# First mixer in a new order, distance biases as stacked fp32r products ahead of both mixers, and input loads on the weight queue

## Chip, cores, metric

The kernel runs on one core of a Trainium2 chip. The metric is the time of one execution in device microseconds; three runs of the kernel before the change gave a median of 3287.96 us. TensorE does the matrix products, VectorE (DVE) and ScalarE (ACT) the elementwise work, GpSimd (POOL) elementwise work and some DMA issues, SyncE (SP) issues the weight loads.

## What is computed

The reference runs two blocks one after the other on one sequence of 256 tokens with 1024 features. The first block has a mixer AB, an expert layer, a mixer C and another expert layer; the second has two gated mixers, each followed by a retrieval layer. The change touches mixer AB and the start of mixer C.

```python
def mixer_ab(x, w_in, gate_b, conv_w, head_g, w_out, rel_bias):
    p = einsum('bsd,de->bse', x, w_in)      # aq ak av (8 heads of 64), bq bk bv bo (4 heads of 128), bi bf
    qk = silu(causal_conv(p[..., AB_BQ:AB_BV], conv_w))
    ya = dilated_attention(aq, ak, av, rel_bias)          # softmax(q k / 8 + bias(distance)) v
    yb = sigmoid(bo) * head_norm(mlstm(bq, bk, bv, bi, bf), head_g)
    return einsum('bse,ed->bsd', concatenate([ya, yb]), w_out)
# mlstm per head, with b = cumsum(log_sigmoid(f)):
#   P = exp(D - m),  D[t,s] = b[t] - b[s] + i[s] for s <= t,  m = max(b + 0, max_s D)
#   h = (q k' * P) v / max(|sum_s (q k' * P)|, exp(-m))
# mixer_c: three attentions over 8 heads; its logits add rel_bias[bucket(distance)] too,
#   those of the compressed keys at the distances t - (16 n + 31), n = 0..14
```

## The kernel before

Every weight product is made in fp32 accuracy from two fp32r parts: a weight tile of 128 x 1024 is loaded by SP into one of three raw buffers (`rawb`), split in halves of 512 columns into a high part (`splitb`, ScalarE, `split_half` at L481) and a low part (`raw - high`, L504, by GpSimd or VectorE, as the field `lo` of `stream_order` says), and TensorE makes three products of each (high-high, high-low, low-high). The five base buffers of split halves form a ring: a half is split when the half five places before it has been used. The order of weight tiles is one list (`stream_order`); each engine's program goes through the stages in the same order, and `fed(n)` in an engine's program splits the halves that the next n tiles free. So the order on each engine is written by hand, and every instruction waits only for counters.

A distance bias (`Bias`) is built by TensorE: the table `relp` (32 buckets and a row of ones), repeated over 128 columns, times a 0/1 matrix `ohm` (33 x 512), plain fp32 operands in `arena`, one product for each of 8 heads. ScalarE copies each to `tmp` (2 buffers), GpSimd writes it to DRAM (`skew`), and one load with a slanted pattern reads it back as `B`. Each mixer does this at its own start, before its first weight product. Mixer C also makes 30 products of 8 columns for the compressed keys (`ohc`, `Bc`).

Mixer AB goes: 16 transposes of x (`Start`), 8 bias products, 8 tiles `aq` (`proj`, 24 products of 256 columns each), 8 tiles `ab_v` (`rows`, 12 products of 512 columns each), the gate inputs (`Narrow`, 48 products), then attention A in 8 steps (score, softmax, transpose, mix, one after the other) with the 8 convolved tiles `bq` between, then the mLSTM in 8 cells of its own chain with the 8 tiles `ab_o` between, the head norm on VectorE, 16 transposes of y and 8 tiles `ab_out`. `aq`, `ab_v`, `bq`, `ab_o` and `ab_out` name tiles below; `hH`, `hL` are high and low parts of the transposed activations. Norm follows, then the expert layer.

Of the kernel before, what the change touches and what calls it, by code (L numbers as in the profile page):

```python
# [25 lines left out]
AB_AUX = dict(conv=32, gateb=8, headg=512, rel=8, wif=64)  # L26
C_AUX = dict(gateb=24, pos=64, rel=8, wg=192)
# [180 lines left out]
def stream_order(dram):  # L208
# [222 lines left out]
class Sync(Lane):  # L431
    def program(self, S):
        group = None
        for n, (src, _, lo, ring) in enumerate(S.order):
# [348 lines left out]
class Start:  # L783


# [3 lines left out]
    def act(self, act):  # L789
        S = self.S  # L790
        act.load("cst", S.cst[:, :], S.dram["consts"])
        act.load("x", S.hrow, S.dram["x_rows"])
        act.load("rt", S.rt[:, :], S.dram["router"])
        for t in range(2):
            take_transposes_act(act, S, t, "xT")

    def dve(self, dve):
        dve.fill(self.S.eps, EPS, ("eps",))
        for t in range(2):
            take_transposes_dve(dve, self.S, t, "xT")  # L800

    def pe(self, pe):
        S = self.S
        pe.wait_ge(S.load("cst"), "cst")
        pe.wait_ge(S.load("x"), "x")
        for t in range(2):
            pe.transposes(S.hrow[:, t, :], t, "xT")

    def pool(self, pool):
        pass  # L810
# [26 lines left out]
class Bias:  # L837


    def __init__(self, S, layer, B, relp, ohm, tmp, table):  # L840
        self.S, self.layer, self.B, self.relp, self.ohm, self.tmp = S, layer, B, relp, ohm, tmp
        self.table = table

    def act(self, act):
        S, n = self.S, self.layer
        for h in range(8):
            act.wait_ge(S.product, "bias", n, h)
            if h >= 2:
                act.wait_ge(S.load(f"skew{n}_{h - 2}"), "skew")
            act.cp(self.tmp[:, h % 2, :], S.bank["bias", n, h], ("bias", n, h), ("drained", ("bias", n, h)))  # L850

    def dve(self, dve):
        dve.fill(self.relp[32:33, :, :], 1.0)
        dve.cp(self.relp[0:32, :, :], bc(self.table, 2, 128), ("rel", self.layer))

    def pe(self, pe):
        S, n = self.S, self.layer
        pe.wait_ge(S.vdone, "rel", n)
        pe.wait_ge(S.load(f"ohm{n}"), f"ohm{n}")
        for h in range(8):  # L860
            b = pe.open("bias", n, h)
            pe.out(pe.mm(b, self.relp[0:33, h, :], self.ohm, True, True), ("bias", n, h))

    def pool(self, pool):
        S, n = self.S, self.layer
        for h in range(8):
            pool.wait_ge(S.acted, "bias", n, h)
            sig = S.load(f"skew{n}_{h}")
            pool.eng.dma_start(S.skew.ap()[n, h, :, :], self.tmp[:, h % 2, :]).then_inc(sig.sem, sig.step(("skew",)))
        for h in range(8):  # L870
            pool.wait_ge(S.load(f"skew{n}_{h}"), "skew")
        sig = S.load(f"B{n}")
        src = bass.AP(S.skew, n * 8 * 65536 + 127, [[511, 128], [65536, 8], [1, 256]])
        pool.eng.dma_start(self.B, src).then_inc(sig.sem, sig.step(("B",)))
# [27 lines left out]
class MixerAB:  # L902
    HEADS = [(h, t) for h in (0, 2, 4, 6) for t in range(2)]
    CELLS = [(h, t) for h in range(4) for t in range(2)]

    def __init__(self, S):
        self.S = S
        R = Room(S.arena)
        self.aux = S.aux_views(AB_AUX)
        self.B = R.get(8, 256)  # L910
        relp = R.get(8, 128)
        self.ohm = R.get(512)
        tmp = R.get(2, 512)
# [8 lines left out]
        self.rcol = R.get(2, 4)  # L922
        self.l2 = [R.get(512) for _ in range(3)]
        self.p2 = [R.get(512) for _ in range(3)]
        self.lp = [R.get(256) for _ in range(4)]
        self.pt = [R.get(256) for _ in range(4)]
        self.dgb = [R.get(256) for _ in range(2)]
        self.small = [R.get(16) for _ in range(8)]
        self.small2 = [R.get(16) for _ in range(8)]
        self.w8 = R.get(2, 4)  # L930
        self.hn = R.get(2, 4, 32)
        self.cmask = R.get(256)
        self.bias = Bias(S, 0, self.B, relp, self.ohm[0:33, :], tmp, self.aux["rel"][0:32, :])
        self.narrow = Narrow(S, self.aux["wif"], 8, "ab.if")

    def pe(self, pe):
        S = self.S
        self.bias.pe(pe)
# [3 lines left out]
        pe.rows(1024, "rows", "ab.v")  # L942
        self.narrow.pe(pe)
        b = pe.open("ab.b")
# [5 lines left out]
        for k, j in steps(8, 3, 8):  # L950
            if k == 0:
                self.pe_score(pe, j)
            elif k == 1:
                self.pe_turn(pe, j)
            elif k == 2:
                self.pe_mix(pe, j)
            else:
                i = CONV[j]
                pe.proj(pe.open("bq", i)[:, 0:256], ("bq", i))
        for t in range(2):  # L960
            pe.wait_ge(S.acted, "ab.v", t, 0)
        for k, j in steps(8, 3, 8):
            if k == 0:
                self.pe_mscore(pe, j)
            elif k == 1:
                self.pe_mturn(pe, j)
            elif k == 2:
                self.pe_mmix(pe, j)
            else:
                pe.row_step(j, 8, 512, "rows", "ab.o")  # L970
        pe.wait_ge(S.vdone, "ab.y")
        for t in range(2):
            pe.transposes(self.y[:, t, :], t, "ab.yT")
        pe.rows_T = ("ab.yT",)
        pe.wait_ge(S.acted, "ab.o", 1)
        pe.rows(1024, "rows", 0)
# [24 lines left out]
    def pe_mix(self, pe, j):  # L1001
        S = self.S
        h, t = self.HEADS[j]
        ns = 128 * (t + 1)
        p = self.p2[j % 3]
        b = pe.open("ab.x", j)
        pe.wait_ge(S.acted, "ab.p", j)
        pe.wait_ge(S.acted, "ab.v", 1, 1)
        for a in range(2):
            for i in range(t + 1):  # L1010
                ins = pe.mm(b[:, 64 * a:64 * a + 64], p[:, ns * a + 128 * i:ns * a + 128 * i + 128],
                            self.vv[:, i, 64 * (h + a):64 * (h + a) + 64], i == 0, i == t)
        pe.out(ins, ("ab.x", j))

    def pe_mscore(self, pe, j):
        S = self.S
        h, t = self.CELLS[j]
        ns = 128 * (t + 1)
        b = pe.open("ml.s", j)
        pe.wait_ge(S.vdone, "ml.d", j)  # L1020
        pe.out(pe.mm(b[:, 0:ns], S.ones, self.dgb[j % 2][:, 0:ns], True, True), ("ml.d", j))
        pe.wait_ge(S.acted, "bqk")
        pe.out(pe.mm(b[:, 256:256 + ns], self.bqk[:, h, 128 * t:128 * t + 128], self.bqk[:, 4 + h, 0:ns],
                     True, True), ("ml.s", j))

    def pe_mturn(self, pe, j):
        S = self.S
        h, t = self.CELLS[j]
        b = pe.open("ml.t", j)
        pe.wait_ge(S.vdone, "ml.w", j)  # L1030
        for i in range(t + 1):
# [1802 lines left out]
```

## Time and profile before

| | us |
|---|---|
| median of 3 runs | 3287.96 (3286.97 to 3293.88) |
| the profiled execution | 3281.58 |
| its span, first to last instruction | 3279.80 |
| of that, from the start to the end of mixer AB | 225.98 |
| of that, mixer C, from its first product to the Norm behind it | 640.59 to 857.80 |

The profiled execution is 6.4 us shorter than the median. Times in the trace count from the first instruction. The granted clock is a share of 2.4 GHz: 1.00 is 2.4, 0.50 is 1.2.

### The profile page before, as it was taken

To read this page: it belongs to the slowest core of one execution; us is meant where nothing else is said; L and a number is where in the kernel's file an instruction comes from. 1 tells how busy PE (TensorE), PEld (TensorE's weight loads), DVE (VectorE), ACT (ScalarE), POOL (GpSimd) and SP (SyncE) were. 2 spreads that over 40 slices of the span, in tenths; PEclk is the share of its full clock that TensorE was granted. 3 is DMA by queue.
4 is the path that set the end of the run, shared out by engine and by line. 5 is a ranking of instruction groups with operands and counts; after the bars stand their busy time and mean duration, and the time that the engine had idled before them with its cause. 6 is when DMAs were issued, how large, how long until landed. Compare 5 with 4: busy or idle time off the path is not lost.

```text
span 3279.8 us, 48648 instructions
## 1 busy us (share of the span) xinstructions
PE 3053.8 (93%) x17834; PEld 2663.9 (81%) x17834; DVE 2214.4 (68%) x3863; ACT 1855.0 (57%) x2824; POOL 1137.7 (35%) x1046
## 2 busy tenths in 40 slices
PE   7769999898899997989999999999989999999998
PEld 6647888586688885789999988887779999988887
DVE  0448999504589995569665557776569855557777
ACT  4446888424578884544555555555555555555554
POOL 6321000132200002569767620001568867630000
PEclk8879999789899998999999999999999999999999
DMA  5237999443489992346665567776345665567775
GB/s 186 71 117 267 370 368 371 177 139 109 160 334 368 372 371 85 103 148 201 192 187 184 183 224 242 242 241 215 104 141 188 204 184 184 181 222 241 242 243 201
DMA packets 203808, 702.01 MB, mean 214 GB/s; under 512 B 23633, under 2 KB 24017, under 8 KB 203155
## 3 DMA queue, kind: packets, MB, share of 16 engines
q1 hardware_dynamic: 170784, 617.69, 56.5%
q10 hardware_dynamic: 20724, 41.36, 3.5%
q0 software_dynamic: 12064, 39.86, 3.1%
q8 instruction: 144, 2.36, 0.3%
q14 instruction: 92, 0.75, 0.1%
HBM read 660.01 MB, written 38.80 MB: 213 GB/s over the span
## 4 chain that ended last, share of the span: by engine, by line
PE 85%; DVE 6%; POOL 3%; ACT 2%; DMA 2%; issue 1%; ACTq 0%; DVEq 0%; SPq 0%; POOLq 0%
PE ps L552 84%; POOL splitb L504 3%; PE ps L563 2%; DVE hrow L104 1%; DVE arena L104 1%; DVE arena L94 1%; ACT splitb L481 1%; DVE arena L99 1%; ACT arena L158 1%; ACT L158 1%; DMA rawb<-in_peer_u 0%; DMA rawb<-in_cmp_w 0%; DVE hL L94 0%; ACT arena L160 0%; DMA rawb<-in_peer_v 0%
## 5 line engine op out<-in xcount | busy, mean ns | idle before, releaser
L481 ACT ACTIVATE splitb<-rawb 128x512 fp32r<-128x512 f32 x1328 | 833.0, 631 | 950.1 <-PE ps L552 795.6
L504 POOL TENSOR_TENSOR splitb<-rawb,splitb 128x512 fp32r<-128x512 f32 x632 | 854.8, 1369 | 1389.2 <-ACT splitb L481 1378.2
L552 PE MATMUL ps<-hH,splitb 128*128 128x256 f32 x5248 | 987.3, 287 | 16.7 <-POOL splitb L504 16.2
L552 PEld LDWEIGHTS ps<-hH,splitb 128*128 128x128 f32 x5248 | 837.6, 194 | 22.5 <-ACT splitb L481 10.6
L552 PE MATMUL ps<-splitb,hid 128*128 128x512 f32 x3444 | 791.9, 390 | 10.8 <-issue 10.8
L552 PEld LDWEIGHTS ps<-splitb,hid 128*128 128x128 f32 x3444 | 648.8, 188 | 147.2 <-issue 11.2
L504 DVE TENSOR_TENSOR splitb<-rawb,splitb 128x512 fp32r<-128x512 f32 x696 | 484.2, 714 | 414.6 <-ACT splitb L481 413.9
L552 PE MATMUL ps<-hL,splitb 128*128 128x256 f32 x2624 | 748.3, 285 | 0.0
L552 PEld LDWEIGHTS ps<-hL,splitb 128*128 128x128 f32 x2624 | 509.6, 194 | 0.0
L552 PE MATMUL ps<-experts_r 128*128 128x512 f32 (+1 forms) x1348 | 332.8, 398 | 14.9 <-ACT experts_r L158 8.5
L552 PEld LDWEIGHTS ps<-experts_r 128*128 128x128 f32 x1348 | 254.9, 196 | 69.9 <-ACT experts_r L158 7.5
L2602 POOL DMA_DIRECT2D aux<-spill x128 | 68.9, 539 | 606.9 <-DVE hid L94 581.3
L504 DVE TENSOR_TENSOR splitb<-experts,splitb 128x1024 fp32r<-128x1024 f32 x188 | 228.0, 1223 | 17.2 <-ACT splitb L481 13.5
L481 ACT ACTIVATE splitb<-experts 128x1024 fp32r<-128x1024 f32 x192 | 202.0, 1059 | 46.2 <-PE ps L552 46.0
L552 PE MATMUL ps<-splitb,hH 128*128 128x512 f32 x640 | 209.6, 410 | 5.5 <-DVE hL L94 5.5
L158 ACT ACTIVATE arena<-ps 128x512 f32<-128x512 f32 (+3 forms) x292 | 152.7, 523 | 106.9 <-PE ps L552 80.6
L552 PE MATMUL ps<-splitb,experts_r 128*128 128x512 f32 x780 | 196.1, 396 | 0.0
L552 PE MATMUL ps<-arena 128*128 128x128 f32 (+8 forms) x896 | 170.2, 342 | 25.4 <-DVE arena L110 8.7
L504 DVE TENSOR_TENSOR experts_r<-experts,experts_r 128x1024 fp32r<-128x1024 f32 x140 | 169.8, 1223 | 23.0 <-ACT experts_r L481 17.9
L504 DVE TENSOR_TENSOR experts_r<-rawb,experts_r 128x1024 fp32r<-128x1024 f32 x144 | 174.8, 1223 | 12.5 <-ACT experts_r L481 6.5
L552 PEld LDWEIGHTS ps<-arena 128*128 128x128 f32 (+3 forms) x896 | 126.0, 217 | 63.4 <-issue 14.9
L481 ACT ACTIVATE experts_r<-experts 128x1024 fp32r<-128x1024 f32 x144 | 151.4, 1059 | 38.5 <-PE ps L552 38.4
(153 smaller groups left out, 3320.1 us busy)
## 6 DMA issues: line engine op xcount, KB each, us to landing
rawb<-in_peer_u SPq DMA_DIRECT2D x256, 512.0 KB, 3.7
rawb<-in_peer_v SPq DMA_DIRECT2D x256, 512.0 KB, 4.2
experts<-in_moe_gu SPq DMA_DIRECT2D x228, 512.0 KB, 5.5
experts<-in_moe_d SPq DMA_DIRECT2D x108, 512.0 KB, 5.4
rawb<-in_moe_gu SPq DMA_DIRECT2D x92, 512.0 KB, 5.4
spill<-gb ACTq DMA_DIRECT2D x128, 256.0 KB, 4.2
aux<-spill POOLq DMA_DIRECT2D x128, 256.0 KB, 4.3
rawb<-in_moe_d SPq DMA_DIRECT2D x52, 512.0 KB, 5.3
```

Source lines behind the costliest of these rows:

```text
L94: self.eng.tensor_tensor(o, a, b, op).then_inc(self.done.sem, self.done.step(*names))
L99: self.eng.tensor_scalar(o, a, s1, s2, op0, op1).then_inc(self.done.sem, self.done.step(*names))
L104: self.eng.scalar_tensor_tensor(out=o, in0=a, scalar=s, in1=b, op0=op0, op1=op1, accum_out=accum).then_inc(self.done.sem, self.done.step(* ...
L158: self.eng.activation(o, a, f, bias=bias, scale=scale).then_inc(self.done.sem, self.done.step(*names))
L481: self.eng.activation(S.split(m)[0], S.raw(n)[:, off:off + w], ACT.Copy).then_inc(S.hi.sem, S.hi.step(("half", m)))
L504: self.eng.tensor_tensor(l, raw, h.bitcast(F32), ALU.subtract).then_inc(self.low.sem, self.low.step(("half", m), *([("raw", n)] if last el ...
L552: return self.eng.matmul(o, w, x, start=start, stop=stop)
L563: return self.eng.transpose(o, a, self.S.ident)
L2602: pool.eng.dma_start(self.hb[i % 3], S.spill.ap()[n, i, :, :]).then_inc(ring.sem, ring.step(("back", i)))
```

## The change

Start: SP, not ScalarE, loads the constants and x (now in two halves), ahead of all weights; the first splits come after the transposes of x, and ScalarE's first load is `aux`. The tiles of `aq` get their low half on VectorE. The bias products take fp32r operands: `rel` stacks the table's rounded high part on rows 0 to 31 and its remainder on rows 32 to 63, with rows of ones at 64 to 96, and `ohm` has 97 rows; each head is still one product. The 8 products for mixer AB stand between the `aq` tiles, the 8 for mixer C between the `bq` tiles of mixer AB; mixer C only reads its `B`, and takes the compressed keys' bias from `B` with a stride of 16, so that `ohc`, `Bc` and their 30 products are gone. Mixer AB's order is now `aq`, gates, `bq`, `ab_v` with the scores and transposes of A, `ab_o` with the mLSTM, `ab_out` in two halves. The mLSTM computes its decays E for all heads at once (`pe_decays`, `dve_decays`, `dve_tops`), without the row shift b[t]; scores of both token tiles share a bank, as do the mixes of all heads; the normalizing factor goes into the head norm.

```diff
 for i in range(8):
-    put(dram["ab_T"][i])
+    put(dram["ab_T"][i], lo="dve")
+for i in CONV:
+    put(dram["ab_T"][8 + i])
 for k in range(8):
     put(dram["ab_v"][k])
-for i in CONV:
-    put(dram["ab_T"][8 + i])
...
 class Sync(Lane):
     def program(self, S):
+        self.load("cst", S.cst[:, :], S.dram["consts"])
+        for t in range(2):
+            self.load(f"x{t}", S.hrow[:, t, :], S.dram["x_rows"][:, t, :])
...
 class Splitter(Lane):
-        self.split_to(0)
...
 class Start:
     def act(self, act):
-        act.load("cst", S.cst[:, :], S.dram["consts"])
-        act.load("x", S.hrow, S.dram["x_rows"])
+        act.load("aux_ab", S.aux[:, 0:places(AB_AUX)[1]], S.dram["ab_aux"])
         act.load("rt", S.rt[:, :], S.dram["router"])
-        for t in range(2):
-            take_transposes_act(act, S, t, "xT")
+        for t, k0 in self.QUARTERS:
+            take_quarter_act(act, S, t, k0, "xT")
+        act.split_to(0)
...
 class Bias:
+    def dve_rel(self, dve):
+        wide = bc(self.table, 2, 128)
+        dve.cp(self.rel[64:97, :, :], bc(self.S.ones[64:97, :], 1, 8))
+        dve.cp(self.rel[0:64, :, :], wide[0:64])
+        dve.tt(self.rel[32:64, :, :], wide[32:64], self.rel[32:64, :, :].bitcast(F32), ALU.subtract)
+    def dve_hot(self, dve):
+        dve.wait_ge(S.load(f"ohm{n}"), f"ohm{n}")
+        dve.cp(self.ohm[0:97, :], self.stage[0:97, :])
+        dve.tt(self.ohm[96:97, :], self.stage[96:97, :], self.ohm[96:97, :].bitcast(F32), ALU.subtract, ("hot", n))
+    def pe(self, pe, h):
+        pe.wait_ge(S.vdone, "hot", n)
+        b = pe.open("bias", n, h)
+        pe.out(pe.mm(b, self.rel[0:97, h, :], self.ohm[0:97, :], True, True), ("bias", n, h))
...
 class MixerAB:
     def pe(self, pe):
-        self.bias.pe(pe)
         for i in range(8):
             pe.proj(pe.open("aq", i)[:, 0:256], ("aq", i))
-        pe.rows(1024, "rows", "ab.v")
+            self.bias[0].pe(pe, i)
         self.narrow.pe(pe)
+        for j, i in enumerate(CONV):
+            pe.proj(pe.open("bq", i)[:, 0:256], ("bq", i))
+            self.bias[1].pe(pe, j)
+            if j == 2:
+                self.pe_sums(pe)
+            elif j == 4:
+                self.pe_decays(pe)
+        for j in range(8):
+            self.pe_score(pe, j)
+            if j:
+                self.pe_turn(pe, j - 1)
+            pe.row_step(j, 8, 1024, "rows", "ab.v")
+        self.pe_mscore(pe, 0)
+        self.pe_turn(pe, 7)
+        self.pe_mscore(pe, 1)
+        pe.wait_ge(S.acted, "ab.v", 1, 1)
+        pe.row_step(0, 8, 512, "rows", "ab.o")
...
+        for k in range(4, 8):
+            pe.row_step(k, 8, 512, "rows", "ab.o")
+        for t in range(2):
+            pe.wait_ge(S.vdone, "ab.ya", t)
+            pe.quarter(self.y[:, t, :], t, 0, "ab.yT")
+        pe.wait_ge(S.acted, "ab.o", 1)
+        for k in range(4):
+            pe.row_step(k, 8, 1024, "rows", 0)
+        for t in range(2):
+            pe.wait_ge(S.vdone, "ab.yb", t)
+            pe.quarter(self.y[:, t, :], t, 4, "ab.yT")
+        self.bias[1].written(pe)
+        for k in range(4, 8):
+            pe.row_step(k, 8, 1024, "rows", 0)
...
     def act(self, act):
+        act.fed(4)
+        act.wait_ge(S.product, "rows", "ab.o")
+        for t in range(2):
+            act.act(self.bo[:, t, :], S.accs[2 * t], ACT.Sigmoid, ("ab.o", t))
+        for t in range(2):
+            take_quarter_act(act, S, t, 0, "ab.yT")
+        act.fed(2)
+        for t in range(2):
+            act.wait_ge(S.vdone, "hn.v", t)
+            act.act(self.hn[:, t, :, 3:4], self.hn[:, t, :, 2:3], ACT.Sqrt, ("hn.s", t))
+        act.fed(2)
+        for t in range(2):
+            take_quarter_act(act, S, t, 4, "ab.yT")
...
 class MixerC:
     def pe(self, pe):
-        self.bias.pe(pe)
-        for t in range(2):
-            b = pe.open("c.bc", t)
-            for n in range(15):
-                ins = pe.mm(b[:, 8 * n:8 * n + 8], oh[0:33, t, n, :], self.relr[0:33, :], True, True)
     def act(self, act):
-        self.bias.act(act)
+        read_bias(act, S, 1, self.B)
     def pool(self, pool):
-        self.bias.pool(pool)
```

VectorE at the start of the program, before the change; the name `arena` holds `relp`, `aux` the table, `nw` the gate weights.

```order
L131 MEMSET st 128x1
L94 TENSOR_TENSOR hL<-ps,hH 128x4x128 x4
L131 MEMSET arena 1x1024
L110 COPY arena<-aux 32x1024
L110 CAST nw<-aux 128x64
L94 TENSOR_TENSOR nw<-aux,nw 128x64
L94 TENSOR_TENSOR arena<-ps,aux 128x16
```

The same place after it; `experts_r` now holds `rel` and `ohm`.

```order
L131 MEMSET st 128x1
L94 TENSOR_TENSOR hL<-ps,hH 128x4x128 x4
L514 TENSOR_TENSOR splitb<-rawb,splitb 128x512 x5
L110 CAST experts_r<-cst 33x1024
L110 CAST experts_r<-aux 64x1024
L94 TENSOR_TENSOR experts_r<-aux,experts_r 32x1024
L110 CAST experts_r<-arena 97x512
L94 TENSOR_TENSOR experts_r<-arena,experts_r 1x512
L514 TENSOR_TENSOR splitb<-rawb,splitb 128x512 x8
```

Five low halves and five steps on `rel` and `ohm` now stand between the transposes of x and the first bias product.

ScalarE at the end of mixer AB before the change, from the last splits of `ab_o` on; the 1024-column ACTIVATE is the sigmoid, that of 8 columns the square root.

```order
L481 ACTIVATE splitb<-rawb 128x512 x2
L158 ACTIVATE arena<-ps 128x512 x2
L158 ACT_TABLE_LOAD
L158 ACTIVATE arena<-arena 128x1024
L158 ACT_TABLE_LOAD
L158 ACTIVATE arena<-arena 128x8
L158 ACTIVATE hH<-ps 128x4x128 x4
L481 ACTIVATE splitb<-rawb 128x512 x11
```

The same place after it; the sigmoid reads PSUM.

```order
L491 ACTIVATE splitb<-rawb 128x512 x5
L158 ACT_TABLE_LOAD
L158 ACTIVATE arena<-ps 128x512 x2
L158 ACTIVATE hH<-ps 128x4x128 x2
L491 ACTIVATE splitb<-rawb 128x512 x4
L158 ACT_TABLE_LOAD
L158 ACTIVATE arena<-arena 128x4 x2
L491 ACTIVATE splitb<-rawb 128x512 x4
L158 ACTIVATE hH<-ps 128x4x128 x2
```

The copies of y's transposes are in two pairs, and four splits for `ab_out` stand before the square root and four behind it.

TensorE at the start of mixer C, before the change.

```order
L563 MATMUL ps<-cst,hrow 128x128 x16
L552 MATMUL ps<-arena 128x512 x8
L552 MATMUL ps<-arena 128x8 x30
L552 MATMUL ps<-hH,splitb 128x256
L552 MATMUL ps<-hL,splitb 128x256
```

And after it.

```order
L573 MATMUL ps<-cst,hrow 128x128 x16
L562 MATMUL ps<-hH,splitb 128x256
L562 MATMUL ps<-hL,splitb 128x256
L562 MATMUL ps<-hH,splitb 128x256 x2
L562 MATMUL ps<-hL,splitb 128x256
```

The 38 products ahead of the first weight product are gone.

## Rows read from the trace of the kernel before

**Rows 1.** The page's busy times, and its chain that ended last, by engine.
```profile
PE 3053.8 (93%) x17834; PEld 2663.9 (81%) x17834; DVE 2214.4 (68%) x3863; ACT 1855.0 (57%) x2824; POOL 1137.7 (35%) x1046
...
PE 85%; DVE 6%; POOL 3%; ACT 2%; DMA 2%; issue 1%; ACTq 0%; DVEq 0%; SPq 0%; POOLq 0%
```

**Rows 2.** Windows by stage to the end of mixer AB: length, busy us, clock.
```profile
0.00:21.77 21.77, 3.42 (x17) 3.21 (x17) 4.44 (x8) 6.60 (x10) 6.33 (x9) 0.95 0.59 216
21.77:35.72 13.95, 13.95 (x17) 5.17 (x17) 0.40 (x2) 4.19 (x7) 3.96 (x7) 0.50 0.30 113
35.72:60.85 25.13, 25.13 (x194) 25.13 (x194) 0.00 (x0) 11.87 (x23) 19.72 (x17) 0.91 0.66 198
60.85:82.63 21.78, 21.78 (x98) 18.02 (x97) 0.00 (x0) 10.40 (x17) 20.81 (x17) 1.00 0.61 189
82.63:88.09 5.46, 5.42 (x49) 5.33 (x47) 0.00 (x1) 2.91 (x5) 2.09 (x2) 1.00 0.48 170
88.09:143.66 55.57, 46.86 (x305) 40.59 (x305) 29.09 (x70) 28.20 (x62) 20.28 (x16) 0.87 0.22 66
143.66:200.28 56.62, 29.40 (x115) 21.05 (x115) 30.89 (x113) 19.04 (x39) 10.16 (x8) 0.74 0.15 48
200.28:225.98 25.70, 25.66 (x112) 21.36 (x112) 4.04 (x8) 9.45 (x16) 14.14 (x11) 0.93 0.35 103
```

**Rows 3.** The chain of work up to 60 us: start, length, what.
```profile
7.30 5.89 DMA hrow<-in_x_rows
...
13.32 2.81 PE ps L563 x12
...
16.86 2.97 DMA aux<-in_ab_aux
...
21.03 0.69 DVE arena L110
```

**Rows 4.** A DMA issue with KB and us; one window, last DMA share and GB/s.
```profile
cst<-in_consts ACTq DMA_DIRECT2D x1, 330.0 KB, 2.9
...
3.00:4.00 1.00, 0.00 (x0) 0.00 (x0) 0.00 (x0) 0.00 (x0) 0.00 (x0) 1.00 1.00 406
```

**Rows 5.** Groups by form: count, busy us, mean ns, idle before.
```profile
L504 POOL TENSOR_TENSOR splitb<-rawb,splitb 128x512 fp32r<-128x512 f32 x24 | 30.4, 1276 | 75.0 <-ACT splitb L481 74.8
L481 ACT ACTIVATE splitb<-rawb 128x512 fp32r<-128x512 f32 x24 | 14.9, 628 | 21.5 <-PE ps L552 20.1 <-DMA rawb<-in_ab_o 1.3
...
L504 DVE TENSOR_TENSOR splitb<-rawb,splitb 128x512 fp32r<-128x512 f32 x696 | 484.2, 714 | 414.6 <-ACT splitb L481 413.9
```

**Rows 6.** TensorE's timeline inside attention A: start, busy, waits.
```profile
105.26 1.45 PE L552 MATMUL ps<-arena 64*128 64x256 f32 x4
106.64 0.44 PE L563 MATMUL ps<-cst,arena 128*128 128x128 f32 x2
```

**Rows 7.** The mLSTM's tail on ScalarE, then TensorE's timeline.
```profile
192.50 1.28 ACT L158 ACT_TABLE_LOAD   x1
193.80 0.22 ACT L158 ACTIVATE arena<-arena 128x8 f32<-128x8 f32 x1
...
200.28 3.67 PE L563 MATMUL ps<-cst,arena 128*128 128x128 f32 x16 [12.06 <-DVE arena L94]
```

**Rows 8.** TensorE's timeline at mixer C's start, and the window before it.
```profile
638.35:640.59 2.24, 0.00 (x0) 0.00 (x0) 1.82 (x4) 0.00 (x0) 0.00 (x0) 0.50 0.70 181
...
640.59 26.62 PE L552 MATMUL ps<-arena 33*128 33x512 f32 x76 [3.69 <-DVE arena L110]
667.14 0.58 PE L552 MATMUL ps<-hH,splitb 128*128 128x256 f32 x1
```

**Rows 9.** Windows that show the clock after a short and a long gap.
```profile
120.00:124.00 4.00, 2.89 (x18) 2.92 (x19) 1.59 (x5) 2.91 (x10) 0.00 (x0) 0.77 0.00 0
...
671.14:675.14 4.00, 4.00 (x33) 4.00 (x33) 0.00 (x0) 1.53 (x3) 2.92 (x3) 0.93 0.39 132
```

**Rows 10.** The chain in mixer C's compression.
```profile
725.92 4.35 DMA rawb<-in_cmp_w
```

More of the change, by code:

```diff
@@ L837 @@
 class Bias:
[L840 to L844, printed above, removed]
-        S, n = self.S, self.layer
[L846 to L856, printed above, removed]
-        S, n = self.S, self.layer
[L858 to L864, printed above, removed]
-        S, n = self.S, self.layer
[L866 to L874, printed above, removed]
+    def __init__(self, S, layer, table, rel, stage, ohm, tmp):
+        self.S, self.layer, self.tmp = S, layer, tmp
+        self.table, self.rel, self.stage, self.ohm = table, rel, stage, ohm
@@ new lines, in pool, with written, read_bias @@
+    def pool(self, pool, h):
+        S, n = self.S, self.layer
+        m = 8 * n + h
+        pool.wait_ge(S.acted, "bias", n, h)
+        sig = S.load(f"skew{m % 4}")
+        pool.eng.dma_start(S.skew.ap()[n, h, :, :], self.tmp[:, h % 4, :]).then_inc(sig.sem, sig.step(("skew", m)))
+    def written(self, lane):
+        for m in range(8 * self.layer + 4, 8 * self.layer + 8):
+            lane.wait_ge(self.S.load(f"skew{m % 4}"), "skew", m)
+def read_bias(lane, S, layer, B):
+    sig = S.load(f"B{layer}")
+    src = bass.AP(S.skew, layer * 8 * 65536 + 127, [[511, 128], [65536, 8], [1, 256]])
+    lane.eng.dma_start(B, src).then_inc(sig.sem, sig.step(("B",)))
@@ L949, in pe, with pe_decays @@
         pe.out(pe.mm(b[:, 4:8], tri[:, 0:128], lg[:, 1, :], False, True), ("ab.b",))
[L950 to L976, printed above, removed]
+    def pe_decays(self, pe):
+        S = self.S
+        pe.wait_ge(S.vdone, "ml.dg")
+        for q in range(2):
+            b = pe.open("ml.d", q)
+            pe.out(pe.mm(b, S.ones, self.dg[:, 512 * q:512 * q + 512], True, True), ("ml.d", q))
     def pe_score(self, pe, j):
@@ L1048, in act @@
-        act.load("ohm0", self.ohm[0:33, :], S.dram["ohm"][0])
+        for n in range(2):
+            act.load(f"ohm{n}", self.stage[n][0:97, :], S.dram["ohm"][n])
         act.load("cmask", self.cmask, S.dram["cmask"])
-        self.bias.act(act)
         for i in range(8):
@@ L1239 @@
+    def pool(self, pool):
+        for i in range(8):
+            self.bias[0].pool(pool, i)
+            pool.fed()
+        for j in range(8):
+            pool.fed()
+            if j == 0:
+                self.bias[0].written(pool)
+                read_bias(pool, self.S, 0, self.B)
+            self.bias[1].pool(pool, j)
+        pool.fed(8 + 8 + 8)
 class MixerC:
@@ L1268, in __init__ @@
         self.small = [R.get(8) for _ in range(16)]
-        self.relr = R.get(8)
-        self.bias = Bias(S, 1, self.B, relp, self.ohm[0:33, :], tmp, self.aux["rel"][0:32, :])
         self.narrow = Narrow(S, self.aux["wg"], 24, "c.g")
@@ L2750, in lay_out @@
     d = {}
[L2751 removed]
+    d["consts"], d["ohm"], d["cmask"], d["lev"] = constants()
     x = i["x"][0]
```

488 lines of the change are left out of this document (256 added, 232 removed).

## The prediction

> **What bounds the kernel now.** I read the page first. TensorE is busy for 93% of the span and holds 85% of the chain that ended last [rows 1], so time is to be had only where TensorE waits, runs at the lower clock, or does products that can go. The windows by stage show where that is in mixer AB: it takes 225.98 us, of which TensorE is idle for 18.35 of the first 21.77 us, 8.7 of the 55.57 us of attention A and 27.2 of the 56.62 us of the mLSTM; and the bias products hold it for 13.95 us at clock 0.50 [rows 2]. At full clock the weight products are cheap beside this: 21.78 us for 8 tiles of 12 products [rows 2], so 0.227 us for 512 columns. The 8 `aq` tiles took 25.13 us at clock 0.91 [rows 2], that is about 23.0 us at 1.00, or 2.88 us a tile.
>
> The chain of work explains the start: x is issued at 7.30 us, because ScalarE first splits five halves, and lands 5.89 us later; behind the transposes the chain goes to the load of `aux` and to VectorE's table [rows 3]. In mixer C the timeline shows 76 records of bias products, 26.55 us from 640.59 to 667.14, and the window of 2.24 us ahead of them holds no product, only VectorE's four steps on the table, behind the last low part of the activations; the clock is low [rows 8].
>
> **Mixer C, removed work.** The first weight product moves from 667.14 to 638.35, where that window begins: 28.8 us. Its five halves are split long before, since GpSimd is idle there. What does it start with? A low clock, as before: 4.0 us after the first weight product the window 671.14:675.14 still has 0.93 [rows 9], and I expect the same rise after the same start, so that cost shifts and does not grow. The load of `B` (1 MB) moves to this place from GpSimd's queue and has over 100 us until the first score, the weight tiles that it delays have three buffers of lead. The strided bias costs VectorE two short steps. What follows is partly bound by loads, as by the 4.35 us wait for a compression tile [rows 10]; those loads are issued as buffers come free, so they shift along. Term: 28.8 us, bounds 25 to 30.
>
> **Mixer AB, moved and rebuilt work.** I build the new time along TensorE.
>
> 1. Start. Ahead of x's first half now stand 330 KB of constants, 512 KB of x, and 492 KB on ScalarE's queue beside them. The stretch 3 to 4 us moved 406 GB/s [rows 4]; with some 2.5 us before data flows at that rate, the first half lands at 6.2 us and the second at 7.4. From x's landing the first 12 transposes took 2.81 us [rows 3]; with the last four, their copy and their low part it was 4.9 us; with a late second half the transposes end near 10, the low parts near 11.3. ScalarE splits only then (0.63 us each), VectorE needs 0.71 us more [rows 5]: first weight product at 12.1 instead of 35.72.
> 2. The new wait. The first bias product stands behind the first tile, and waits for VectorE: five low halves of 0.714 us [rows 5] from 11.4 to 15.0, then five steps on `rel` and `ohm`. The trace has no such steps; the copy of 32 x 1024 took 0.69 us [rows 3], a subtraction of 512 columns about 0.7. That bounds the five between 3.2 and 5 us; I take 4, so 19.0. What is queued behind the wait is all of TensorE's work; what is lost is 19.0 minus the first tile's end at 15 to 17. Then seven tiles and eight bias products: 7 x 2.88 + 8 x 0.23 = 22.0 us, where I price an fp32r product of 97 rows as a 512-column weight product (bounds 0.23, and 13.95/8 = 1.74, what the fp32 ones took at half clock). With 2 us for the low clock: 43.0. Before: 60.85.
> 3. Gates, unchanged: 5.46 us [rows 2]: 48.5.
> 4. `bq`: 8 x (2.88 + 0.23) + 0.7 for the sums + 1.9 for the decays (512 columns fp32; scores of 256 took 1.38 us the pair [rows 6]) = 27.5: 76.0. The cover: GpSimd makes two low halves of 1.28 to 1.37 us and issues one write of 0.54, at most 3.3 us a tile against 3.4 on TensorE. VectorE has 8 x 2.0 us of convolution and some 7 us of decays. Neither binds, but GpSimd only just.
> 5. `ab_v` with scores: 21.8 + 4 x 1.38 + 4 x 0.96 for scores + 2.6 for transposes = 33.8: 109.8. The softmax of step j (VectorE 1.4, ScalarE 1.2 us) lies under a row step of 2.72 plus the next score. ScalarE has up to 4.0 us of work per 4.2.
> 6. mLSTM and `ab_o`: mLSTM scores 3.5, last turn 0.4, `ab_o` 8 x 1.36 = 10.9, mixes of A 5.3, turns 1.3, mLSTM mixes 3.3, and one wait of 2.2 until ScalarE has copied four banks of `ab_v` (0.6 us each): 26.9, and 1 us of clock: 137.7. Call it z. Before, this stretch was a chain of small steps across three engines.
> 7. Tail. After z ScalarE does one split 0.63, a table load 1.28, two sigmoids and two copies of 0.6; VectorE 0.7: `ab_out` starts at z + 4.5. Four tiles to z + 15.4. ScalarE's four splits ahead of the square root wait for the second of these tiles (z + 9.9), then 0.6 + 1.28 [rows 7] + 0.25: z + 12.1; VectorE's two outputs of 3.0 us end at z + 18.2, the last transposed low part at z + 20.2. So TensorE stalls for about 4 us in the middle of `ab_out`, and ends at z + 30.4. Before, the same join held it for 12.06 us [rows 7].
> 8. The clock after gaps. A gap of 1.5 us in attention A was followed by a mean of 0.77 over the next 4 us [rows 9] and the same over 4 more, so each of the two tail gaps costs about 2 us at half speed: 4 us. Sum: 137.7 + 30.4 + 4 = 172.
>
> Gain in AB: 226 - 172 = 54 us. If no gap lowers the clock and the wait in step 2 vanishes: 161, gain 65. If GpSimd or ScalarE binds in steps 4 and 5 (1 us a tile, 16 us more): gain 38.
>
> The Trainium skill (ScalarE: Activation LUTs, What ACT_TABLE_LOAD costs) says that a change of table costs a drain of about 1380 ns beside the load of 1283 ns. The row speaks against it: the load at 192.50 ends at 193.78 and the activation begins at 193.80 [rows 7]. By the rule the two loads of the tail would add 2.8 us and mixer AB would end at 175; I go by the row.
>
> The same skill (TensorE: Matmul & The Clock Gate, Part 1) says that the throttled clock is the default and activity releases it. The bias products were 26.55 us without a gap and the clock stayed at 0.50 [rows 2, 8], so being busy alone did not release it here; the page would have let one expect otherwise.
>
> **Sum.** 28.8 + 54 = 82.8 us. The profiled execution of 3281.58 would become 3198.8, the median of 3287.96 would become 3205.2. I say 3204. The rest of the program, from 226 to 638 us and from 860 us on, keeps its instructions and their order.
>
> **Rivals.**
> - *A hand-off binds in the rebuilt mixer* (0.15): GpSimd at 3.3 us a tile, or ScalarE at 4.0 of 4.2 us, falls behind, or the split ring runs dry after the wait of step 2. For it: both margins are under 0.3 us. Against: five halves of lead. 16 to 30 us more: 3221 to 3235.
> - *More than forecast* (0.06): the clock stays high and the five steps are short; AB at 161 or less, 3194 and under, down to 3185.
> - *Mixer C's gain is absorbed* (0.04): the earlier start meets loads that don't move. Against: the raw buffers are full at 638 and the waits [rows 10] follow TensorE's own use. Half of it lost gives 3219.
> - *Slower, by the clock* (0.02): bias products in plain fp32 with 33 rows kept TensorE at 0.50 through 14 and 26.6 us. If such products, now strewn between the tiles of `aq`, `bq` and with the 64-row scores in `ab_v`, hold the clock at 0.50 there, the 83 us of steps 2, 4 and 5 take 83 us more and the gain is nil; it decides only from there, with all three stages low, and with the added waits gives 3290 to 3300. Against: attention A ran at full clock with 64-row scores in it [rows 6], and the bias is 0.23 of 3.1 us.
> - *The change does nothing* (0.01): not possible for TensorE's removed 26.55 us unless the above holds.
>
> **Chances.** The forecast has 0.72; its own range is 3191 to 3218, from the bounds above with 3 us for the clock and 3 us for the median. With rivals the range of 8 in 10 is 3190 to 3225. No difference means within 0.2%, 6.6 us. Faster 0.97, same 0.01, slower 0.02.
>
> **What will show it.** In the changed profile: first weight product at 12 us; a wait of TensorE on VectorE of 2 to 4 us near 15 to 19; no window of half clock beyond 5 us after the first tiles; mixer AB's last product at 172 us against 225.98; the stretch of `ab_v` with scores at 34 us; two gaps of 3 to 5 us around the first half of `ab_out`; mixer C's first weight product 2.3 us or less after its last transposed copy. It is wrong if GpSimd's low halves or ScalarE are named as what TensorE waited for in `bq` or `ab_v`, or if the expert layer behind the mixer, 248 to 625 us before, changes its length.

## Result, and the profile after the change

The changed kernel takes 3216.96 us, the median of 4 runs (3210.64 to 3219.93), against 3290.11 for the kernel before beside it: the ratio is 0.9775, 95% interval 0.9755 to 0.9794. A second comparison gave 3215.49 (5 runs) against 3286.39 (9 runs), ratio 0.9785 (0.9771 to 0.9798). That is 73 and 71 us less; 3204 us and a gain of 82.8 us were forecast. The profiled execution took 3217.93 us.

The page's busy times and chain by engine, which answer to [rows 1]:

```profile
PE 3014.8 (94%) x17746; PEld 2641.0 (82%) x17746; DVE 2221.1 (69%) x3818; ACT 1849.8 (58%) x2819; POOL 1118.2 (35%) x1029
...
PE 84%; DVE 6%; POOL 4%; ACT 3%; DMA 2%; issue 1%; ACTq 0%; DVEq 0%; SPq 0%; POOLq 0%
```

TensorE is busy for 39.0 us less; the other 24.7 us by which the span is shorter are idle time that went. The windows of mixer AB by its new stages (length, busy us and instructions of PE, PEld, DVE, ACT, POOL, clock, DMA share, GB/s), beside [rows 2]:

```profile
0.00:13.92 13.92, 3.90 (x16) 3.16 (x17) 3.82 (x7) 5.39 (x9) 0.19 (x4) 1.00 0.69 249
13.92:26.79 12.87, 4.34 (x25) 4.04 (x25) 5.75 (x10) 2.30 (x5) 0.00 (x0) 0.69 0.32 109
26.79:51.36 24.57, 24.57 (x177) 24.19 (x177) 8.85 (x15) 14.04 (x26) 5.89 (x9) 0.89 0.60 202
51.36:57.00 5.64, 5.64 (x50) 5.64 (x48) 0.00 (x0) 1.50 (x3) 4.98 (x5) 0.94 0.60 212
57.00:89.66 32.66, 30.91 (x212) 28.47 (x212) 22.52 (x43) 18.30 (x33) 24.40 (x24) 0.91 0.64 211
89.66:123.90 34.24, 33.78 (x146) 23.77 (x147) 10.82 (x20) 25.34 (x65) 18.89 (x16) 1.00 0.36 109
123.90:150.54 26.64, 24.09 (x156) 21.34 (x155) 9.59 (x43) 11.06 (x21) 10.64 (x9) 1.00 0.31 96
150.54:187.66 37.12, 28.88 (x113) 22.59 (x111) 11.70 (x25) 13.91 (x23) 17.02 (x13) 0.86 0.29 95
```

The rows are: to the first weight product; the first tile and the wait for the first bias product; the other `aq` tiles; the gates; `bq`; `ab_v` with the scores; the mLSTM with `ab_o`; the tail. Mixer AB ends at 187.66 us against 225.98, a gain of 38.3. Its worst row is the second: 8.5 of 12.87 us idle. The chain there, start, length and what:

```profile
12.51 13.05 DMA arena<-in_ohm
25.56 0.02 issue
25.58 0.44 DVE experts_r L110
26.02 0.02 issue
26.04 0.70 DVE experts_r L94
26.74 0.04 issue
26.79 33.29 PE ps L562 x237
```

The load of the 0/1 matrix `ohm`, 194 KB, takes 13.05 us. From 19 to 24 us, while it is still under way, the 16 DMA engines are busy for a mean share of 0.09 only, as much as 1.4 of them would make (the last two numbers of the window are that share and GB/s):

```profile
19.00:24.00 5.00, 0.00 (x0) 0.00 (x0) 0.00 (x0) 0.00 (x0) 0.00 (x0) 0.82 0.09 37
```

The load also holds the engine that issues it. ScalarE's timeline: the issue that follows the two `ohm` loads lasts 10.83 us, and the next split has waited 9.72 us for it.

```profile
13.64 10.83 ACTq L499 DMA_DIRECT2D arena<-in_cmask  x1
...
24.52 1.15 ACT L491 ACTIVATE splitb<-rawb 128x512 fp32r<-128x512 f32 x2 [9.72 <-issue]
```

Mixer C, measured from the first transpose of the Norm ahead of it to that of the Norm behind it, takes 205.1 us (591.62 to 796.72) against 232.5 (630.00 to 862.51): 27.4 us less. The windows behind its first weight product, beside [rows 9], show the rise of the clock that was expected:

```profile
598.50:602.50 4.00, 4.00 (x21) 4.00 (x21) 1.75 (x4) 1.23 (x2) 0.57 (x1) 0.51 0.73 167
602.50:606.50 4.00, 4.00 (x35) 4.00 (x35) 0.00 (x0) 1.84 (x4) 3.11 (x3) 1.00 0.86 283
```

### The profile page after: what moved, and what is told of

It reads as the page before. It is cut to its first block, busy times and chain, and to the rows that moved or that the text cites. A ratio compares the mean times of both kernels' runs of the same rounds, so it can differ in the third digit from the quotient of the medians.

```text
span 3216.1 us, 48380 instructions
## 1 busy us (share of the span) xinstructions
PE 3014.8 (94%) x17746; PEld 2641.0 (82%) x17746; DVE 2221.1 (69%) x3818; ACT 1849.8 (58%) x2819; POOL 1118.2 (35%) x1029
## 4 chain that ended last, share of the span: by engine, by line
PE 84%; DVE 6%; POOL 4%; ACT 3%; DMA 2%; issue 1%; ACTq 0%; DVEq 0%; SPq 0%; POOLq 0%
PE ps L562 82%; POOL splitb L514 4%; PE ps L573 1%; DVE arena L94 1%; DVE hrow L104 1%; DVE arena L104 1%; ACT splitb L491 1%; DMA rawb<-in_peer_u 1%; ACT arena L158 1%; ACT L158 1%; DVE arena L99 0%; DMA arena<-in_ohm 0%; DVE hL L94 0%; DMA rawb<-in_cmp_w 0%; ACT arena L160 0%
## 5 line engine op out<-in xcount | busy, mean ns | idle before, releaser
L514 POOL TENSOR_TENSOR splitb<-rawb,splitb 128x512 fp32r<-128x512 f32 x616 | 836.6, 1375 | 1352.0 <-ACT splitb L491 1342.6
L514 DVE TENSOR_TENSOR splitb<-rawb,splitb 128x512 fp32r<-128x512 f32 x712 | 494.5, 712 | 427.0 <-ACT splitb L491 425.9
L562 PE MATMUL ps<-experts_r 128*128 128x512 f32 (+2 forms) x1364 | 338.8, 397 | 23.9 <-ACT experts_r L158 9.0
L562 PEld LDWEIGHTS ps<-experts_r 128*128 128x128 f32 (+1 forms) x1364 | 256.9, 195 | 79.3 <-DVE experts_r L94 9.8
L562 PEld LDWEIGHTS ps<-splitb,experts_r 128*128 128x128 f32 x780 | 145.1, 188 | 33.6
L491 ACT ACTIVATE experts_r<-rawb 128x1024 fp32r<-128x1024 f32 x144 | 151.8, 1061 | 34.2 <-PE ps L562 33.9
```

The source lines that it names most:

```text
L491: self.eng.activation(S.split(m)[0], S.raw(n)[:, off:off + w], ACT.Copy).then_inc(S.hi.sem, S.hi.step(("half", m)))
L514: self.eng.tensor_tensor(l, raw, h.bitcast(F32), ALU.subtract).then_inc(self.low.sem, self.low.step(("half", m), *([("raw", n)] if last el ...
L562: return self.eng.matmul(o, w, x, start=start, stop=stop)
```

## The experiments

Each kernel is the changed kernel with the edit shown; only the last section repeats the two kernels as they are. I compare mostly where a stage ends in the profile, since that repeats better than the whole time (last experiment).

### Is it the number of rows?

97 is a prime. These three kernels change the number of rows or the moment of the load.

```diff
-    ohm = np.zeros((2, 97, 512), np.float32)
+    ohm = np.zeros((2, 128, 512), np.float32)
...
-            act.load(f"ohm{n}", self.stage[n][0:97, :], S.dram["ohm"][n])
+            act.load(f"ohm{n}", self.stage[n][0:128, :], S.dram["ohm"][n])
```

> The 0/1 matrix gets 31 rows of zeros, so that its two loads have 128 rows instead of 97; nothing else changes. Theory (the number of rows decides how many DMA engines share the load): the first load lands 2 to 5 us after it begins at 12.5 us instead of 13.05, the first bias product comes at 19 us instead of 26.79, ScalarE's second issue no longer holds it for 10.83 us, and mixer AB ends near 180 instead of 187.66. Rival (the load is late because the queues are full of weights and x): 128 rows land no earlier than 25 us, and AB ends at 187 to 188.

> The same with 112 rows, which 16 divides as it does 128. Theory (rows divided over 16 engines): like 128 rows, landing before 18 us and AB ending near 180. Rival (only a full 128 rows are spread): like 97 rows, landing near 25 us, AB ending at 187 to 188.

> 97 rows as before, but ScalarE issues both loads right behind that of the aux table, ahead of the copies of x's transposes. Theory (slow for its rows, 13 us from issue): begun near 3 us, it lands at 15 to 17 us, and the first bias product stands at 19 to 20 us; the second load and the router's then hold ScalarE's queue, which delays the copies of the transposes if an issue blocks the engine, by up to 10 us: then no gain. Rival (late for its issue alone): it lands within 5 us, at 8, and nothing is held; AB ends near 180.

The two `ohm` loads with 128 rows, as the page's part on DMA issues has them (KB each, median us from issue to landing), and the first bias product on TensorE's timeline:

```profile
arena<-in_ohm ACTq DMA_DIRECT2D x2, 256.0 KB, 2.9
```

```profile
19.71 0.50 PE L562 MATMUL ps<-experts_r 97*128 97x512 f32 x1 [1.54 <-DVE experts_r L94]
```

With 112 rows, where the first bias product stood at 19.74:

```profile
arena<-in_ohm ACTq DMA_DIRECT2D x2, 224.0 KB, 3.0
```

More bytes land in under a quarter of the time. The first bias product comes 7.1 us earlier, and what holds it now is VectorE; mixer AB ends at 178.47 with 128 rows. The two kernels were timed once each, 3202.00 and 3201.06. Issued early with 97 rows, the load pays elsewhere. ScalarE's timeline:

```profile
1.18 5.09 ACTq L499 DMA_DIRECT2D arena<-in_ohm  x2
6.30 11.76 ACTq L499 DMA_DIRECT2D rt<-in_router  x1
```

ScalarE is held until 18.06, its copies of x's transposes start at 19.39 instead of 8.57, the first weight product comes at 24.06 and the first bias product at 30.09, not at 19 to 20. AB ends at 188.86 (time 3221.16). When the early load lands can't be seen here, since nothing waits for it. What decides are the loads of 112 and 128 rows: issued at the same place as the one of 97, they land in 3 us. So the load is slow for its rows, not late, and the rival of a full queue falls.

The Trainium skill (DMA: Bandwidth & Descriptors, Why a DMA increments its semaphore by 16 and not by 1) says that a transfer is cut over the largest number of engines, up to 16, that divides its outermost size, and that 127 rows get one engine. By it 97 rows, a prime, get one, and 112 and 128 get 16. The times of the three runs agree (13.05, 3.0 and 2.9 us), and so does the low share of the DMA engines above; no run counts the engines one by one. I had not weighed it for this load.

Is the 8 us beyond AB, which both single times show, the edit's too?

> The kernel with the matrix in 128 rows, in five rounds. Theory: its one profile gained 9.2 us in AB and 8 us behind mixer C, and only the 9 us are its own, so the median is 8 to 10 us under that of the changed kernel in the same call, near 3208. Rival (the 8 us behind mixer C belong to it too): 15 to 17 us under.

It is not: the median of 5 runs is 3207.02, 8.5 us under the 3215.49 of the changed kernel on the same chip (ratios to before 0.9756, 0.9741 to 0.9771, and 0.9785, 0.9771 to 0.9798). AB ended at 180.19.

### The bias products: format and clock

```diff
-        pe.out(pe.mm(b, self.rel[0:97, h, :], self.ohm[0:97, :], True, True), ("bias", n, h))
+        pe.out(pe.mm(b, self.rel[0:97, h, :].bitcast(F32), self.ohm[0:97, :].bitcast(F32), True, True), ("bias", n, h))
```

> The 16 bias products read the same stacked operands as plain fp32. Theory: one such product costs four passes of 512 columns, 0.87 us at full clock (13.95 / 8 = 1.74 at 0.50 before the change), against about 0.4 with overlap for fp32r, so 16 x 0.5 to 0.65 = 8 to 10 us more in AB, the clock in bq and ab_v stays at 1.00, and AB ends at 195 to 198. Rival (plain fp32 products hold the clock at 0.50): bq stands at over 55 us instead of 32.7, AB ends beyond 215. Third: AB's slow first tiles are at half clock anyway, so there each costs 1.7 us, 5 us more again.

The end of `ab_o` came 7.7 us later (158.29 for 150.54), the tail took as long as before (37.3 for 37.1), and AB ended at 195.6, 7.9 us later and at the lower end of the theory. The single time was 3221.70. The gates and the stretch of `bq` (the columns of the windows above):

```profile
56.20:63.45 7.25, 7.25 (x50) 7.01 (x49) 0.00 (x0) 1.30 (x3) 4.13 (x4) 0.77 0.60 181
63.45:97.41 33.96, 33.96 (x220) 28.86 (x220) 21.21 (x45) 18.38 (x31) 23.83 (x23) 0.95 0.57 194
```

The clock is 0.95 in `bq`, so plain fp32 products of 97 rows between the tiles do not hold it down, and neither does anything in `ab_v`, at 1.00. What the rival "slower, by the clock" feared did not come even in this format. The stretch of `bq` grew by 1.3 us only, but part of the low clock now lies in the gates before it (7.25 us for 5.64). Both together took 41.2 us for 38.3, so the format costs 2.9 us here: TensorE is busy for 4.7 us more, and 1.8 us of that fill the waits that the changed kernel has in `bq`. The eight products between the `aq` tiles cost 4.9 us more (29.5 for 24.6), since there nothing waits.

Mixer C's 27.4 us come from three things: products dropped, format, place of the rest. Two kernels put its 8 bias products back at its own start, still stacked, with the compressed keys read from `B`. In the first the operands lie in `arena`, which is plain fp32, so its text on record is wrong where it says fp32r: it measures stacked plain fp32 products. In the second they are fp32r. Both have 128 rows in the load.

```diff
 class MixerC:
     def pe(self, pe):
+        for h in range(8):
+            self.bias.pe(pe, h)
...
     def dve(self, dve):
+        self.bias.dve_rel(dve)
+        self.bias.dve_hot(dve)
...
```

> Mixer C's bias stands at its own start again, ahead of its first weight product, but as stacked fp32r products and with the matrix in 128 rows; the compressed keys still read it from B. To be compared with the run with 128 rows (mixer C, transposes to transposes, 205.4 us there and 205.1 in the changed kernel). Theory (half of C's 27.4 us came from the format and the strided reading, the other half from the place): the load, VectorE's 3.7 us of steps behind the low parts and 8 products of 0.43 at a clock of 0.50 to 1.0 give 7 to 11 us more, so C at 212 to 216; mixer AB is 3 to 5 us shorter, without 8 products and what surrounds them; the time is 3205 to 3210. Rival (the format gives nothing, only moving does): C back at 228 to 232.

> As the run before with mixer C's bias at mixer C's start, but with its operands written as fp32r, which that run's were not (its products were plain fp32: 9.8 us for 8). Theory: 8 products of 0.43 to 0.6 us, 3.4 to 5, behind the same wait of 5.4 us: mixer C at 213 to 215 instead of 219.1, so that fp32r is worth 5 us here and the place 8 to 9. Rival (the products take as long, held by the low clock): 218 to 219.

TensorE's timeline in the first and in the second:

```profile
593.60 10.37 PE L562 MATMUL ps<-arena 97*128 97x512 f32 x16 [5.43 <-DVE arena L94]
603.40 0.68 PE L562 MATMUL ps<-hH,splitb 128*128 128x256 f32 x1
```

```profile
594.50 4.42 PE L562 MATMUL ps<-experts_r 97*128 97x512 f32 x8 [5.43 <-DVE experts_r L94]
599.29 0.58 PE L562 MATMUL ps<-hH,splitb 128*128 128x256 f32 x1 [0.37 <-ACT arena L158]
```

Mixer C took 219.1 us (581.26 to 800.36) and 214.5 us (582.17 to 796.67): the first missed its 212 to 216, the second met its 213 to 215. The times, one each, were 3219.83 and 3213.41, both above the 3205 to 3210 expected of the first. From 232.5 down: 13.4 us for the 30 small products and what went with them, 4.6 us for the format, and 9 to 12 us for the place (205.1 and 202.2 us in the two profiles of the changed kernel). Mixer AB gave back little for it: it ends at 175.9 and 178.1 without mixer C's products, against 178.5 and 180.2 with them.

### The clock behind the gates

```diff
-        for i in range(8):
+        def tile(i):
             pe.proj(pe.open("aq", i)[:, 0:256], ("aq", i))
             self.bias[0].pe(pe, i)
-        self.narrow.pe(pe)
+
+        for i in range(7):
+            tile(i)
+        self.narrow.pe(pe, lambda: tile(7))
```

`Narrow.pe` calls what it is given between its two token tiles.

> The 48 products of the gates (8 columns each, 5.6 us) are made in two halves, with the last aq tile and its bias product between them; nothing else changes. Before, after and the three runs so far all have a clock near 0.50 in the 4 us behind the gates, though TensorE has no gap there. Theory (the run of small products itself lowers the clock): two runs of 2.8 us with 3.3 us of full products between lower it for less time or not at all; the stretch from the gates' first product to the first score falls from 38.3 us (less the 3.1 us of the tile moved into it, so 41.4 to compare) by 2 to 3 us, and mixer AB ends at 185 to 186. Rival (the clock falls for another reason, such as the load that other engines put on the chip at that moment): it falls at the same time as before, AB ends at 187 to 188. A third outcome, each half drawing a fall of its own, would give 190.

The windows behind the gates in the changed kernel:

```profile
56.00:60.00 4.00, 4.00 (x21) 4.00 (x22) 0.34 (x2) 0.10 (x1) 0.36 (x1) 0.54 0.41 135
60.00:64.00 4.00, 4.00 (x23) 3.90 (x22) 1.45 (x3) 1.65 (x3) 2.06 (x2) 0.61 0.22 60
```

and with the gates in two halves, there and 70 us on:

```profile
56.00:60.00 4.00, 4.00 (x23) 4.00 (x23) 1.95 (x2) 0.32 (x1) 2.85 (x3) 0.57 0.50 156
60.00:64.00 4.00, 4.00 (x35) 3.96 (x34) 1.93 (x4) 2.07 (x4) 3.42 (x3) 1.00 0.43 117
...
128.00:132.00 4.00, 4.00 (x14) 3.35 (x13) 0.88 (x7) 0.63 (x1) 1.27 (x1) 0.60 0.04 15
```

The fall costs 4 x 0.43 = 1.7 us instead of 3.4, and the first score comes at 87.94, 1.7 us before the first profile of the changed kernel and 0.9 before its second. But that is not the edit's for certain. The kernel `c_late` above makes all 48 products in one row, and its fall was as short:

```profile
44.00:48.00 4.00, 4.00 (x34) 4.00 (x34) 0.32 (x2) 0.00 (x1) 3.05 (x3) 0.90 0.67 210
48.00:52.00 4.00, 4.00 (x26) 4.00 (x25) 0.03 (x1) 0.63 (x1) 0.87 (x1) 0.67 0.27 110
```

And in the kernel that has all edits (below) the two halves drew two falls (windows at 0.52 and 0.66), 5.1 us in all, and the first score came 1.1 to 1.5 us later than with 128 rows alone. So whether the row of small products lowers the clock is not shown by this pair, and the edit is worth nothing that can be told: the end of AB was 187.5, as if nothing had been done. The third window shows why here. A wait of 2.5 us behind `ab_v`, which left the clock at 1.00 in the changed kernel's first profile, now was followed by a fall. The same wait was followed by one in 6 of the 12 profiles of the changed kernel and its variants, in its own second profile and both with 128 rows among them, and by none in the other 6.

### The tail

```diff
-        act.fed(4)
-        act.wait_ge(S.product, "rows", "ab.o")
-        for t in range(2):
-            act.act(self.bo[:, t, :], S.accs[2 * t], ACT.Sigmoid, ("ab.o", t))
-        for t in range(2):
-            take_quarter_act(act, S, t, 0, "ab.yT")
-        act.fed(2)
+        act.fed(3)
         for t in range(2):
             act.wait_ge(S.vdone, "hn.v", t)
             act.act(self.hn[:, t, :, 3:4], self.hn[:, t, :, 2:3], ACT.Sqrt, ("hn.s", t))
-        act.fed(2)
+        act.fed()
+        act.wait_ge(S.product, "rows", "ab.o")
+        for t in range(2):
+            act.act(self.bo[:, t, :], S.accs[2 * t], ACT.Sigmoid, ("ab.o", t))
+        for t in range(2):
+            take_quarter_act(act, S, t, 0, "ab.yT")
+        act.fed(4)
```

> ScalarE makes the two square roots of the head norm ahead of the last split before the sigmoid, not behind four splits of ab_out. Theory (the 4.13 us wait in the middle of ab_out is VectorE's output, 7.7 us that begin only when the square root is done at 165): the square root comes at about 151, the sigmoid's table load 1.8 us later than now, so ab_out begins at 157.3 instead of 155.5; VectorE's outputs begin by 159 and end by 167, ahead of the fourth tile's end at 169.5; the transposes follow without a wait and ab_out goes on at 172 instead of 175.3, at full clock; AB ends at 181 to 184 instead of 187.66. Rival (the two table loads and the later sigmoid cost what the shorter wait gives): 187 to 189.

AB ended at 183.1 and the tail, from the end of `ab_o` to that of `ab_out`, took 33.0 us. It took 35.8 to 37.3 us in the ten profiles that leave the square root where it was, so the edit is worth 3 to 4 us. The single time, 3210.53, is as short as the shortest of the changed kernel and shows nothing by itself. Both gaps on TensorE's timeline of the changed kernel:

```profile
155.53 1.19 PE L562 MATMUL ps<-splitb,hH 128*128 128x512 f32 x2 [3.95 <-DVE hL L94]
...
172.72 1.11 PE L573 MATMUL ps<-cst,arena 128*128 128x128 f32 x4 [4.13 <-DVE arena L94]
```

and behind the second place with the square root early:

```profile
171.79 0.70 PE L562 MATMUL ps<-splitb,hH 128*128 128x512 f32 x2 [1.21 <-DVE hL L94]
```

The 4.13 us wait is gone, as the theory says; it was ScalarE's square root, queued behind four splits. The first gap grew by 0.9 us, less than the 1.8 I expected.

Everything together, with two more moves in the order of TensorE and ScalarE:

```diff
-        for k in range(4, 8):
+        for k in (4, 5):
             pe.row_step(k, 8, 512, "rows", "ab.o")
         for t in range(2):
             pe.wait_ge(S.vdone, "ab.ya", t)
             pe.quarter(self.y[:, t, :], t, 0, "ab.yT")
+        for k in (6, 7):
+            pe.row_step(k, 8, 512, "rows", "ab.o")
...
-        for k in range(4):
+        for k in range(3):
             pe.row_step(k, 8, 1024, "rows", 0)
         for t in range(2):
             pe.wait_ge(S.vdone, "ab.yb", t)
             pe.quarter(self.y[:, t, :], t, 4, "ab.yT")
+        pe.row_step(3, 8, 1024, "rows", 0)
...
```

> Four edits together: the matrix in 128 rows; the gates' products split around the last aq tile; y's first transposes between the sixth and the seventh tile of ab_o, their copies before the sigmoid, the square root right behind the sigmoid; the last transposes ahead of the fourth tile of ab_out. Theory (each tail gap is the chain behind one late step of ScalarE): the gap behind ab_o falls from 4.0 to about 2.6 us, that in ab_out from 4.1 us to nothing, its clock drop goes with it, and the tail from ab_o's end to ab_out's takes 26 to 28 us against 37.1 and 35.8; AB ends at 167 to 170, the median is 3195 to 3200. Rival (the clock falls elsewhere when a gap goes, as it did behind the split gates): AB ends at 171 to 175.

The window of its tail, and the one wait that is left in it:

```profile
143.65:170.11 26.46, 24.56 (x104) 19.91 (x104) 12.61 (x22) 12.05 (x21) 17.25 (x13) 0.94 0.37 120
```

```profile
145.55 0.72 PE L562 MATMUL ps<-splitb,hH 128*128 128x512 f32 x2 [1.90 <-ACT arena L158]
```

AB ends at 170.11, 17.5 us before the changed kernel's first profile, and the median of 5 runs is 3198.57, 16.9 us under the changed kernel (ratio to before 0.9724, 0.9708 to 0.9740, clear of 0.9785 and its interval). The tail and the median lie inside the theory, AB's end 0.1 us above it. This kernel does not separate what each of its four edits gave. By the runs above 7 to 9 us are the rows of the load and the split of the gates gave nothing that can be told; the tail is 6.5 us shorter than with the early square root alone, which leaves that to the moved transposes, with whatever the clock added. It is the fastest kernel of the study.

### What repeats and what doesn't

> The changed kernel once more, in five rounds with a second profile. Theory (the stages of mixers AB and C repeat, and what lies between them and behind them varies by a few us a run): AB ends at 187 to 188, mixer C takes 202.5 to 205.5 us, and the stretch behind mixer C differs by up to 8 us from the 2421.2 of the first profile; median 3214 to 3219. Rival (the stages themselves vary by as much): AB's end moves by more than 3 us.

> The kernel before once more, for a second profile. Theory (the stages repeat, and the 6 to 10 us by which the first profile lies under the median are behind mixer C or between the mixers): mixer AB ends within 1 us of 225.98 and mixer C takes 230 to 233 us, while the stretch behind it differs from 2422 by several us. Rival: AB's end or mixer C moves by over 3 us, so that the gains read from one pair of profiles are uncertain by as much.

| us | before, twice | changed, twice |
|---|---|---|
| mixer AB's end | 225.98, 227.98 | 187.66, 187.11 |
| from there to the Norm ahead of mixer C | 404.0, 404.0 | 404.0, 404.9 |
| mixer C | 232.5, 232.2 | 205.1, 202.2 |
| all behind it | 2419.1, 2421.5 | 2421.2, 2418.0 |

The theories hold, if not to the digit: the end of mixer AB repeats within 2.0 us (1 us was expected for the kernel before), mixer C within 3, and the long rest moves by 2 to 3 us here, by up to 9 us over all profiles (2413.2 in the first with 128 rows, 2422.4 with the early square root), whatever the edit. One profile stands apart: in the kernel with all four edits mixer C took 208.9 us, though no edit touches it. So a difference of 3 us in mixer C, seen in one pair of profiles, may be no difference.

## Why the prediction was right in sign and range, and forecast 10 us too much

- **Mixer C, 28.8 us.** Right: 27.4 from the first pair of profiles, 30.0 from the second. The first weight product comes 6.7 us behind the Norm's first transpose where it came 37.1 us behind: 30.5 us earlier, 1.7 more than forecast, since it does not wait for the last low part of the activations. The clock is at 0.51 for some 4 us behind it and then at 1.00, as after the old start.
- **Step 1, start.** 13.92 for 12.1: x's halves landed 1.3 us later than I had put them (7.45 and 8.71 us), and the rest is the chain of copies and splits behind them.
- **Step 2, the new wait: the step that failed.** I had the bias product wait for VectorE until 19.0. VectorE had made its low halves and three of the five steps by 18.6; the last two had no input yet. The sum has no term for the `ohm` load at all: neither its bytes nor its rows stand in it (the 492 KB on ScalarE's queue are `aux` and the router's table). It cost 7.1 us, and held ScalarE for 10 us. With 112 or 128 rows the product came at 19.7: the rest of the step was right. The tiles behind it took 24.6 us for 24.0.
- **Steps 3 and 4.** 5.64 for 5.46 and 32.7 for 27.5. The clock was at 0.54 and 0.61 for 8 us while TensorE had no gap; that is 4 x 0.46 + 4 x 0.39 = 3.4 us. One of the prediction's signs, no half clock beyond 5 us after the first tiles, failed here. The other 1.8 us are waits for VectorE, which the prediction said would not bind; its steps of the decays took 0.70 to 1.68 us. The rival "a hand-off binds" named GpSimd and ScalarE; neither did.
- **Steps 5 and 6.** 34.2 for 33.8, 26.6 for 27.9. Right; the wait of 2.2 us was 2.55.
- **Steps 7 and 8, the tail.** 37.1 for 34.4 with the clock. The two gaps are where they were said to be, 3.95 and 4.13 us. The terms of step 7 up to `ab_out` add up to z + 5.0, not z + 4.5, and it began at z + 5.0. The square roots were done at z + 14.7 for z + 12.1, since the clock was 0.66 and 0.91 in the windows from 154 to 162, and VectorE's outputs took 7.7 us for 6.0.

So 7.8 us to the first bias product, 5.9 up to the first score, 2.7 in the tail, less 0.8 in between, make the 15.7 us between 172 and 187.66 but for rounding. That the times show 71 to 73 us gained where the two pairs of profiles show 66 and 71 in both mixers is the spread of the rest: the one profiled execution of before was 8.5 us under the median of the four. The range held, even the forecast's own one of 3191 to 3218, but in part by luck: its upper end was made of allowances for the price of a bias product, for the clock and for the median, and the price of that load was in none of them.

The rule on the table load was rightly set aside: the load at 163.45 takes 1.28 us and the square root begins at 164.75, without the 1380 ns that the Trainium skill (ScalarE: Activation LUTs, What ACT_TABLE_LOAD costs) adds.

## What to carry to other kernels

Count the rows of every load that a moved instruction waits for, not only its KB: make them a multiple of 16, if with zeros, and look at what stands behind its issue on the queue. When a step is moved ahead of work that used to hide its inputs, list every input with its landing time. On a tail that joins three engines, find the one late small step (here a square root behind four splits) before counting the large ones. And where the clock may fall, price a range: behind the same wait of 2.5 us it fell in 6 of 12 profiles.

## What the hardware showed that I had not expected

- A load of 97 rows and 194 KB took 13.05 us, one of 112 rows and 224 KB 3.0 us. The issue of a third load behind two of 97 rows held ScalarE for 10.83 us, and for 11.76 us in the early variant, where the issue of the second of the two took 4.52 us already.
- The clock fell during or behind the 48 products of 8 columns in all 12 profiles of the changed kernel and its variants, to 0.54 in the changed kernel, with TensorE busy throughout. In the kernel before it fell there too, but there TensorE also waits behind the gates (busy for 1.48 of the 4 us from 88 to 92 us). What makes it fall stays open. The Trainium skill (TensorE: Matmul & The Clock Gate, Part 1) ties the clock to how busy the engine is; here busy time alone did not keep it.
- A step of VectorE took longer while GpSimd worked. The same multiplication, 0.69 us when GpSimd had nothing to do, took 1.66 us beside its low halves. VectorE's timeline in the changed kernel, then GpSimd's:

```profile
156.21 0.69 DVE L94 TENSOR_TENSOR arena<-arena,aux 128x512 f32<-128x512 f32 x1
...
167.74 1.66 DVE L94 TENSOR_TENSOR arena<-arena,aux 128x512 f32<-128x512 f32 x1
```

```profile
165.86 4.66 POOL L514 TENSOR_TENSOR splitb<-rawb,splitb 128x512 fp32r<-128x512 f32 x3 [1.05 <-ACT splitb L491]
```

The Trainium skill (SBUF — State Buffer, Who interferes with whom) has the rule: an operation of VectorE with two inputs in SBUF contends with one of GpSimd that reads SBUF. The 0.97 us more fit a wait for the rest of a low half of 1.3 us; no run here takes GpSimd's work away to show it.
